# Two chained sequence-mixing layers on one core: another order inside the delta heads and the HGRN heads

## The chip, the cores and the metric

The kernel is one program on 1 core of a Trainium2 chip. The metric is the device time of one execution in microseconds. Three runs of the kernel before gave 3632.32, 3632.64 and 3636.35 us, a median of 3632.64 us.

## The reference, cut to what matters

Two blocks run one after the other on x of 512 tokens by 2048 channels, in float32.

The first block normalizes x and projects it to 12 groups of a gated delta rule (one query and key head each, two value heads each), a small cross attention over 256 memory rows (4 heads of 256) and gates. A short causal convolution and SiLU make q, k and v:

```python
qkv = jax.nn.silu(causal_depthwise_conv(p[..., :c_qkv], conv_w))
m = jnp.where(strict, beta[..., :, None] * kk * decay, 0.0) + jnp.eye(C)
sol = lax.linalg.triangular_solve(m, rhs, ...)        # u0, w
# over the chunks: u = u0 - w S;  o = q_dec S + (qk * decay) u;  S = cd * S + k_dec^T u
o = rms_norm(o, out_g); y = concatenate([mix, xa]) * silu(z); x = x + y @ w_out
```

The second block projects the normalized x to 4 mLSTM heads and 8 HGRN heads. An HGRN head is

```python
f_b = lb + (1 - lb) * sigmoid(hg_f);  logf = log(f_b);  k_b = (1 - lb) * sigmoid(-hg_f)
b = cumsum(logf);  A[t, j] = sum_e q[t, e] k[j, e] exp(b[t, e] - b[j, e])   for j <= t
o = A v + (q * exp(b)) S;   S = exp(g) * S + (k * exp(g - b))^T v
y_b = rmsnorm(o, hg_norm_w) * silu(hg_g)
```

An output projection, a gated embedding of p and a last norm end the block.

## The kernel before, in words

Activations lie transposed, channels on the 128 partitions and the 512 tokens on the free axis. Each weight tile is 2048 x 128. A projection of one tile is 16 parts (`gemm`, lines 379 to 395); a part is three 128x512 products, since weights and activations are cut into a high and a low half (lines 390, 391, 392). GpSimd cuts the weights of the next tiles (lines 358, 366), SyncE loads them. Tiles alternate between two PSUM banks, `gemm_ps`; a bank is free again when VectorE or ScalarE has moved the result out ("evict").

The work of a head ("mix") is woven into the projection of the next head's tiles. The function `interleave` makes one list of steps: each step has a weight, and it comes before the part at which the sum of the weights ahead of it is due. TensorE, VectorE and ScalarE all walk the same list, each in its own order of queue, and meet over semaphores. A step that waits on one engine holds up all that is behind it on that engine.

A delta head has 6 tiles (q, k, v, v, z, z; 96 parts) and the steps of `DN_STEPS`. "natural" transposes k and makes the products k k and k q; "values" transposes v; "transposed" turns the first inverse block. Then a block inverse is built in levels 1 to 6. Each level has a "half" (TensorE writes bankA, line 523; ScalarE copies it to T1) and a "whole" (TensorE writes bankB and bankC, lines 533 and 535; VectorE merges them with predicated copies, line 798), for each of the two value heads a = 0, 1. Whole 0 of level 1 also waits for `kd` and `ke`, which VectorE makes in its step "transposed". "solved" (lines 542, 547), four pairs "rest" and "output" (the chunks) and "head_out" follow. In "head_out" ScalarE squares the output, TensorE sums the squares of o and of q with a matrix of ones (lines 580, 581), ScalarE takes the square root, and VectorE divides and gates. ScalarE evicts tile c of q, k, v with a scaled copy, VectorE adds the three other taps of the convolution, and ScalarE then applies SiLU (`dn_trip` of ScalarE, from line 1646). The loop runs 11 heads; the last head is woven into the first six tiles of the output projection.

An HGRN head has 4 tiles (f, q, i, g; 64 parts) and the steps of `HG_STEPS`: a diagonal (line 685), levels 0 to 6 (VectorE makes exponents, ScalarE exponentiates in place in bankB, VectorE multiplies by q and k, TensorE multiplies, line 692, VectorE merges, line 1287), "hg_state" (transposes of kdt, line 703), "hg_mix" (line 709), "hg_next" (gates of the next head) and "hg_out" (lines 716, 718, 722). The loop runs 7 heads; the last is woven into two tiles of the second output projection.

The helper `op` of each engine is one line, so VectorE's operations are at line 792 and ScalarE's at line 1454. Table loads that the program asks for are at lines 1588, 1635 and 1829; others, at 1454, are put in by the compiler.

## Time and profile before

| | |
|---|---|
| median of the timed runs | 3632.64 us |
| the profiled execution, its own time | 3633.32 us |
| its span | 3631.5 us |
| TensorE busy | 3369.6 us, 93% |
| VectorE busy | 1534.2 us, 42% |
| ScalarE busy | 846.3 us, 23% |
| GpSimd busy | 1686.3 us, 46% |
| mean granted clock | 0.975 |

Engines in the rows: PE is TensorE's products, PEld its weight loads, DVE is VectorE, ACT ScalarE, POOL GpSimd. A row of a timeline begins with its start and its length in microseconds from the span's start; "x8" means eight instructions put together, and the square bracket gives how long the engine was idle before and what ended that. The ends of matmuls are modelled, so rows of PE overlap. A granted clock of 1.00 is 2.4 GHz, 0.50 is 1.2 GHz.

### The profile page before, as it was taken

Reading aid. Unit: us, or ns where it says so; the run is one execution under the profiler, and the core shown is the slowest. Engines: PE = TensorE matmul, PEld = TensorE weight load, DVE = VectorE, ACT = ScalarE, POOL = GpSimd, SP = SyncE. Lnnn points to the kernel's source line nnn. Section 1 sums busy time; section 2 is a strip of 40 time slices with the busy share of each in tenths; the row PEclk is TensorE's granted clock in tenths of the full one; section 3 lists DMA queues with packets and bytes.
Section 4 is the critical chain, followed back from the end, with each engine's and each line's share of the span. In section 5 each row is a group of like instructions: output and inputs, shape, how many; then the busy total and the mean of one; then the engine's idle time right before and its main releaser. Section 6 shows DMA issues by size and latency. Waiting matters only on the chain.

```text
span 3631.5 us, 47399 instructions
## 1 busy us (share of the span) xinstructions
PE 3369.6 (93%) x17232; PEld 2785.8 (77%) x17232; DVE 1534.2 (42%) x2049; ACT 846.3 (23%) x1269; POOL 1686.3 (46%) x1748
## 2 busy tenths in 40 slices
PE   8999989999999999999899998999988888879896
PEld 7777778788878877887688787777867777658685
DVE  7622244444543444444431214243355555531423
ACT  5412223322332233223310102111122322310111
POOL 0255623443343334334326666666644545437574
PEclk9999999999999999999899999999999999989998
DMA  6322211211111112112214223222222121232222
GB/s 235 117 82 87 93 53 52 69 60 50 64 69 58 52 64 69 41 63 69 93 64 174 81 97 134 87 104 92 92 76 73 64 72 61 98 115 100 73 100 81
DMA packets 53523, 306.68 MB, mean 84 GB/s; under 512 B 5044, under 2 KB 7220, under 8 KB 21844
## 3 DMA queue, kind: packets, MB, share of 16 engines
q1 hardware_dynamic: 33984, 247.48, 19.4%
q10 hardware_dynamic: 19476, 58.32, 4.3%
q8 instruction: 45, 0.74, 0.1%
q14 instruction: 18, 0.15, 0.0%
HBM read 284.74 MB, written 21.04 MB: 84 GB/s over the span
## 4 chain that ended last, share of the span: by engine, by line
PE 76%; DVE 12%; ACT 6%; issue 4%; DMA 1%; ACTq 0%; DVEq 0%; POOL 0%; POOLq 0%
PE gemm_ps L390 19%; PE gemm_ps L392 19%; PE gemm_ps L391 19%; DVE arena L792 8%; DVE arena L798 3%; ACT arena L1454 3%; PE bankC L535 3%; PE bankA L523 3%; PE bankB L533 2%; PE bankA L692 1%; ACT L1454 1%; PE bankB L580 1%; PE bankB L581 1%; DVE a_lo L792 1%; ACT a_hi L1454 1%
## 5 line engine op out<-in xcount | busy, mean ns | idle before, releaser
L390 PE MATMUL gemm_ps<-a_hi,w_hi 128*128 128x512 f32 (+1 forms) x3744 | 1512.2, 404 | 59.4 <-DVE a_lo L792 48.3
L392 PE MATMUL gemm_ps<-a_hi,w_lo 128*128 128x512 f32 (+1 forms) x3744 | 1446.7, 386 | 0.0
L391 PE MATMUL gemm_ps<-a_lo,w_hi 128*128 128x512 f32 (+1 forms) x3744 | 1444.3, 386 | 0.0
L366 POOL CAST w_hi<-w_raw 128x512 fp32r<-128x512 f32 x872 | 536.8, 658 | 1898.4 <-issue 1754.4
L358 POOL TENSOR_TENSOR w_lo<-w_raw,w_hi 128x512 fp32r<-128x512 f32 x872 | 1153.3, 1353 | 4.3
L390 PEld LDWEIGHTS gemm_ps<-a_hi,w_hi 128*128 128x128 f32 x3744 | 713.6, 191 | 216.2 <-issue 47.5
L392 PEld LDWEIGHTS gemm_ps<-a_hi,w_lo 128*128 128x128 f32 x3744 | 711.5, 190 | 143.5
L391 PEld LDWEIGHTS gemm_ps<-a_lo,w_hi 128*128 128x128 f32 x3744 | 714.3, 191 | 129.9 <-issue 10.1
L792 DVE TENSOR_TENSOR arena<-gemm_ps,arena 128x512 f32<-128x512 f32 (+3 forms) x145 | 96.0, 662 | 705.5 <-PE gemm_ps L392 699.4
L792 DVE RECIPROCAL arena<-arena 128x512 f32<-128x512 f32 (+2 forms) x70 | 172.8, 2468 | 352.2 <-ACT arena L1454 350.1
L1454 ACT ACTIVATE arena<-arena 128x512 f32<-128x512 f32 (+5 forms) x334 | 204.4, 612 | 404.3 <-DVE arena L792 390.9
L792 DVE TENSOR_TENSOR arena<-arena 128x512 f32<-128x512 f32 (+4 forms) x219 | 214.4, 979 | 66.5 <-ACT arena L1729 43.9
L535 PE MATMUL bankC<-arena 128*128 128x128 f32 x1152 | 210.9, 275 | 0.0
L523 PE MATMUL bankA<-arena 128*128 128x128 f32 x1152 | 161.5, 283 | 38.5 <-DVE arena L798 19.4
L523 PEld LDWEIGHTS bankA<-arena 128*128 128x128 f32 x1152 | 141.8, 192 | 71.6 <-DVE arena L798 46.5
L1454 ACT ACT_TABLE_LOAD x105 | 134.7, 1283 | 235.8 <-DVE arena L792 200.2
L533 PE MATMUL bankB<-arena 128*128 128x128 f32 x960 | 185.1, 274 | 0.0
L798 DVE COPY_PREDICATED arena<-con,bankB 128x512 f32<-128x512 uint32 x120 | 88.1, 734 | 225.9 <-PE bankC L535 222.9
L1454 ACT ACTIVATE arena<-bankA 128x512 f32<-128x512 f32 x144 | 86.2, 599 | 400.6 <-PE bankA L523 400.6
L535 PEld LDWEIGHTS bankC<-arena 128*128 128x128 f32 x1152 | 170.9, 192 | 2.1
L792 DVE SCALAR_TENSOR_TENSOR arena<-gemm_ps,arena 128x511 f32<-128x511 f32 x144 | 107.8, 748 | 142.6 <-ACT arena L1454 139.2
L533 PEld LDWEIGHTS bankB<-arena 128*128 128x128 f32 x960 | 154.5, 191 | 10.5
(155 smaller groups left out, 2238.2 us busy)
## 6 DMA issues: line engine op xcount, KB each, us to landing
w_raw<-w_stream SPq DMA_DIRECT2D x236, 1024.0 KB, 4.8
y_scratch<-arena ACTq DMA_DIRECT2D x20, 512.0 KB, 3.2
arena<-y_scratch ACTq DMA_DIRECT2D x15, 512.0 KB, 3.7
arena<-gc_scratch ACTq DMA_DIRECT2D x12, 512.0 KB, 3.5
arena<-x_t ACTq DMA_DIRECT2D x2, 2048.0 KB, 10.5
arena<-y_scratch ACTq DMA_DIRECT2D x1, 4096.0 KB, 25.5
x_scratch<-arena ACTq DMA_DIRECT2D x1, 4096.0 KB, 12.1
y_out<-arena ACTq DMA_DIRECT2D x4, 1024.0 KB, 3.9
```

Source lines behind the costliest of these rows:

```text
L358: return pool.tensor_tensor(part(w_lo, w, q), part(w_raw, w, q), part(w_hi, w, q).bitcast(F32), ALU.subtract)
L366: pool.tensor_copy(part(w_hi, w, q), part(w_raw, w, q)).then_inc(pool_step, 1)
L390: pe.matmul(o, hi, a_hi[:, k, 0:width], start=(k == 0), stop=False)
L391: pe.matmul(o, hi, a_lo[:, k, 0:width], start=False, stop=False)
L392: last = pe.matmul(o, lo, a_hi[:, k, 0:width], start=False, stop=(k == KT - 1))
L523: last = pe.matmul(quad(bankA)[:, a, n, :], NmT[:, a, n, :], X[:, a, n, :], start=True, stop=True)
L533: pe.matmul(quad(bankB)[:, a, n, :], XT[:, a, n, :], T1[:, a, n, :], start=True, stop=True)
L535: last = pe.matmul(quad(bankC)[:, a, n, :], T1[:, a, n, :], XT[:, a, n, :], start=True, stop=True)
L580: pe.matmul(bankB[:, a, :], ones, sqr[:, a, :], start=True, stop=False)
L792: d.did(make(*args), sem, value)
L798: d.did(make(*args), sem, value)
L1454: d.did(act.activation(dst, src, func, **kw), sem, value)
```

## The change

In the delta heads the weights of a level's four steps change, and with them their place: the second half comes one part later, directly ahead of whole 0. In "head_out" TensorE first adds the sums of q's squares for both a, without a wait, and then those of o. ScalarE holds the SiLU of an evicted tile back until the next step of the head is done (or, in "head_out", until the two squares are issued), and asks for the Sqrt table after the squares and no longer before them.

In the HGRN heads VectorE holds the eviction of a tile back until the next step is done, except that it comes first where the next step is "hg_next". The exponents of the state (h_b at a chunk's end minus h_b), their Exp on ScalarE and the product kdt move from inside "hg_state" to level 6 and to the start of "hg_state". The SiLU of the gate moves from the end of the head to the start of "hg_next", and ScalarE asks for the Exp table right after the square root of "hg_out".

```diff
-            + [(s, l, a, 0.75) for l in range(1, LEVELS) for s in ("half", "whole") for a in range(2)]
+            + [(s, l, a, w) for l in range(1, LEVELS)
+               for s, a, w in (("half", 0, 2), ("half", 1, 0), ("whole", 0, 1), ("whole", 1, 0))]
...
                 elif step[0] == "head_out":
                     for a in range(2):
+                        pe.matmul(bankB[:, a, :], ones, q_sq, start=True, stop=False)
+                    for a in range(2):
                         pe.wait_ge(s["o_sq"], 2 * j + a + 1)
-                        pe.matmul(bankB[:, a, :], ones, sqr[:, a, :], start=True, stop=False)
-                        pe.matmul(bankB[:, a, :], ones, q_sq, start=False, stop=True).then_inc(s["o_sum"], 1)
+                        pe.matmul(bankB[:, a, :], ones, sqr[:, a, :], start=False, stop=True).then_inc(s["o_sum"], 1)
...
+                    if l == LEVELS - 1:
+                        b3, p3 = h_bs.rearrange(blocks, n=NB), h_b.rearrange(blocks, n=NB)
+                        op(v.tensor_tensor, h_x[1].rearrange(blocks, n=NB), b3[:, :, P - 1:P].to_broadcast([P, NB, P]),
+                           p3, ALU.subtract, sem=s["h_kx"], value=j + 1)
                     v.wait_ge(s["h_ex"], LEVELS * j + l + 1)
...
                 elif step[0] == "hg_state":
+                    v.wait_ge(s["h_kxe"], j + 1)
+                    op(v.tensor_tensor, h_kdt, h_k, h_x[1], ALU.mult, sem=s["h_kdr"], value=j + 1)
                     merge(LEVELS - 1, j)
...
+            def hg_trip(g, j):                       # VectorE
+                held = None
+                for step in interleave(4, HG_STEPS):
                     if step[0] == "evict":
-                        hg_evict(step[1], g)
+                        held = step[1]
                     elif step[0] != "gemm":
+                        if step[0] == "hg_next" and held is not None:
+                            hg_evict(held, g)
+                            held = None
                         hg_mix(step, j, g)
+                        if held is not None:
+                            hg_evict(held, g)
+                            held = None
+                if held is not None:
+                    hg_evict(held, g)
...
+            def conv_silu(c, g):                     # ScalarE
+                slot, n = tile_at(W_DN, c, g, 6)
+                act.wait_ge(evicted[slot], n + 1)
+                op(cv[:, c, :], cv[:, c, :], ACT.Silu, s["silu"], 4 * g + c + 1)
...
                 elif step[0] == "head_out":
-                    act.preload_act_table(ACT.Sqrt)
                     act.wait_ge(s["o"], j + 1)
                     for a in range(2):
                         op(sqr[:, a, :], bankC[:, a, :], ACT.Square, s["o_sq"], 2 * j + a + 1)
+                    if held is not None:
+                        conv_silu(held, g)
+                    act.preload_act_table(ACT.Sqrt)
...
-                        act.wait_ge(evicted[slot], n + 1)
-                        op(o, o, ACT.Silu, s["silu"], 4 * g + c + 1)
+                        held = c
                     elif step[0] not in ("gemm", "evict"):
-                        dn_mix(step, j, g)
+                        dn_mix(step, j, g, held)
+                        if held is not None and step[0] != "head_out":
+                            conv_silu(held, g)
+                        held = None
...
-                if step[0] == "hg_next" and g is not None:
+                if step[0] == "hg_next":             # ScalarE
+                    if j is not None:
+                        slot, n = tile_at(W_HG, 3, j, 4)
+                        act.wait_ge(evicted[slot], n + 1)
+                        op(h_gate, hg_in, ACT.Silu, s["h_gs"], j + 1)
+                    if g is None:
+                        return
...
+                    if step[1] == LEVELS - 1:
+                        act.wait_ge(s["h_kx"], j + 1)
+                        op(h_x[1], h_x[1], ACT.Exp, s["h_kxe"], j + 1)
                 elif step[0] == "hg_state":
-                    act.wait_ge(s["h_kx"], j + 1)
-                    op(h_x[1], h_x[1], ACT.Exp, s["h_kxe"], j + 1)
                     act.wait_ge(s["h_kT"], j + 1)
...
                     op(h_rt, bankA[:, 0, :], ACT.Sqrt, s["h_ort"], j + 1, bias=eps[:, :], scale=1.0 / P)
+                    if g is not None:
+                        act.preload_act_table(ACT.Exp)
...
-                if tiles:
-                    slot, n = tile_at(W_HG, 3, g, 4)
-                    act.wait_ge(evicted[slot], n + 1)
-                    op(h_gate, hg_in, ACT.Silu, s["h_gs"], g + 1)
```

## Rows read from the trace of the kernel before

**Rows 1.** The page, part 1: busy time and share of the span.

```profile
PE 3369.6 (93%) x17232; PEld 2785.8 (77%) x17232; DVE 1534.2 (42%) x2049; ACT 846.3 (23%) x1269; POOL 1686.3 (46%) x1748
```

**Rows 2.** Windows: delta, then HGRN; busy per engine, PE clock, DMA share, GB/s.

```profile
425.00:1790.00 1365.00, 1293.24 (x7583) 1097.00 (x7582) 616.57 (x857) 395.87 (x649) 502.48 (x528) 0.98 0.17 60
...
2702.00:3158.00 456.00, 405.69 (x1959) 331.64 (x1960) 253.14 (x415) 119.28 (x159) 206.65 (x216) 0.97 0.19 67
```

**Rows 3.** TensorE's waits: releaser, total us, times, longest.

```profile
PE bankA L692 <- DVE arena L792: 29.9, 18, 2.1
PE bankB L580 <- ACT arena L1454: 29.0, 11, 2.6
PE bankB L703 <- DVE arena L792: 22.1, 8, 2.8
PE bankA L523 <- DVE arena L798: 19.4, 60, 0.7
PE bankA L523 <- ACT arena L1454: 19.1, 11, 5.1
```

**Rows 4.** Timeline of TensorE at a delta head's end.

```profile
660.03 1.58 PE L580 MATMUL bankB<-arena,con 128*128 128x512 f32 x2 [2.64 <-ACT arena L1454]
661.41 1.91 PE L581 MATMUL bankB<-arena,con 128*128 128x512 f32 x2
...
664.87 0.79 PE L390 MATMUL gemm_ps<-a_hi,w_hi 128*128 128x512 f32 x1
```

**Rows 5.** Timeline of ScalarE at the same place.

```profile
657.44 0.63 ACT L1454 ACTIVATE arena<-arena 128x512 f32<-128x512 f32 x1 [2.55 <-DVE arena L792]
658.09 1.28 ACT L1635 ACT_TABLE_LOAD   x1
659.38 1.23 ACT L1454 ACTIVATE arena<-bankC 128x512 f32<-128x512 f32 x2
```

**Rows 6.** Windows, columns as in rows 2: behind two waits, and undisturbed.

```profile
660.60:664.00 3.40, 3.40 (x6) 1.34 (x5) 0.00 (x0) 0.65 (x2) 1.00 (x1) 0.50 0.38 82
664.00:684.00 20.00, 20.00 (x87) 16.07 (x86) 10.61 (x7) 9.25 (x15) 7.83 (x8) 1.00 0.16 52
...
2806.80:2811.90 5.10, 5.10 (x18) 4.07 (x17) 0.93 (x1) 0.60 (x1) 3.30 (x3) 0.67 0.12 16
```

**Rows 7.** Timeline of TensorE in levels 1 to 4 of a delta head.

```profile
586.74 0.38 PE L533 MATMUL bankB<-arena 128*128 128x128 f32 x2
...
591.00 1.06 PE L523 MATMUL bankA<-arena 128*128 128x128 f32 x8
...
593.00 1.16 PE L523 MATMUL bankA<-arena 128*128 128x128 f32 x8 [0.25 <-DVE arena L798]
...
598.96 0.28 PE L523 MATMUL bankA<-arena 128*128 128x128 f32 x1
...
607.73 0.49 PE L523 MATMUL bankA<-arena 128*128 128x128 f32 x2 [0.65 <-DVE arena L798]
```

**Rows 8.** Timeline of VectorE ahead of level 1; last, in the first head.

```profile
580.29 3.27 DVE L792 TENSOR_TENSOR arena<-arena 128x8 f32<-128x8 f32 x2
583.60 2.48 DVE L792 TENSOR_TENSOR arena<-bankB,arena 128x1024 f32<-128x1024 f32 x2
...
455.77 1.42 DVE L792 TENSOR_TENSOR arena<-arena 128x8 f32<-128x8 f32 x2
```

**Rows 9.** Timeline of TensorE in HGRN: level 0, level 3.

```profile
2838.95 0.49 PE L692 MATMUL bankA<-arena 128*128 128x128 f32 x2 [2.06 <-DVE arena L792]
...
2853.22 0.60 PE L692 MATMUL bankA<-arena 128*128 128x128 f32 x3 [1.94 <-DVE arena L792]
```

**Rows 10.** Timelines of VectorE and ScalarE in HGRN.

```profile
2832.08 0.69 DVE L792 TENSOR_TENSOR arena<-arena 128x512 f32<-128x512 f32 x1
...
2835.39 1.28 ACT L1454 ACT_TABLE_LOAD   x1
...
2849.23 0.58 ACT L1454 ACTIVATE bankB<-bankB 128x512 f32<-128x512 f32 x1
```

More of the change, by code:

```diff
@@ L1336, in hg_mix @@
                                         else h_par[:, bass.ds(j, 1), 2:3].rearrange("p h c -> p (h c)")))
-                    b3, p3 = h_bs.rearrange(blocks, n=NB), h_b.rearrange(blocks, n=NB)
-                    op(v.tensor_tensor, h_x[1].rearrange(blocks, n=NB), b3[:, :, P - 1:P].to_broadcast([P, NB, P]), p3,
-                       ALU.subtract, sem=s["h_kx"], value=j + 1)
-                    v.wait_ge(s["h_kxe"], j + 1)
-                    op(v.tensor_tensor, h_kdt, h_k, h_x[1], ALU.mult, sem=s["h_kdr"], value=j + 1)
                     v.wait_ge(s["h_ebx"], j + 1)
@@ L1357, in hg_mix @@
                     op(v.tensor_tensor, h_y, h_rt, h_gate, ALU.mult, sem=s["h_yr"], value=j + 1)
-            def hg_trip(g, j, tiles=True, mix=True):
-                for step in interleave(4 if tiles else 0, HG_STEPS if mix else []):
+            def hg_trip(g, j):
+                held = None
+                for step in interleave(4, HG_STEPS):
                     if step[0] == "evict":
-                        hg_evict(step[1], g)
+                        held = step[1]
                     elif step[0] != "gemm":
+                        if step[0] == "hg_next" and held is not None:
+                            hg_evict(held, g)
+                            held = None
                         hg_mix(step, j, g)
+                        if held is not None:
[3 more added lines that the diff above has]
+                    hg_evict(held, g)
             v.sem_inc(s["h_yst"], 16)
@@ L1603, in store_head, with dn_mix @@
                 act.dma_start(y_rows.rearrange("a p t -> p a t"), yo[:, :, :]).then_inc(s["dy_stored"], 16)
-            def dn_mix(step, j, g=None):
+            def conv_silu(c, g):
+                slot, n = tile_at(W_DN, c, g, 6)
+                act.wait_ge(evicted[slot], n + 1)
+                op(cv[:, c, :], cv[:, c, :], ACT.Silu, s["silu"], 4 * g + c + 1)
+            def dn_mix(step, j, g=None, held=None):
                 if step[0] == "natural":
@@ L1646, in dn_trip @@
             def dn_trip(g, j, mix=True):
+                held = None
                 for step in interleave(6, DN_STEPS if mix else []):
                     if step[0] == "evict":
+                        if held is not None:
+                            conv_silu(held, g)
+                            held = None
                         c = step[1]
@@ L1659, in dn_trip @@
                         op(o, gemm_ps[slot][:, :], ACT.Copy, s["tapped"], 4 * g + c + 1, scale=cw[:, 4 * c + 3:4 * c + 4])
-                        act.wait_ge(evicted[slot], n + 1)
-                        op(o, o, ACT.Silu, s["silu"], 4 * g + c + 1)
+                        held = c
                     elif step[0] not in ("gemm", "evict"):
-                        dn_mix(step, j, g)
+                        dn_mix(step, j, g, held)
+                        if held is not None and step[0] != "head_out":
+                            conv_silu(held, g)
+                        held = None
                 if not mix:
@@ L1856, in hg_mix, with hg_trip @@
                     act.dma_start(y_row.rearrange("a p t -> p (a t)"), h_y).then_inc(s["h_yst"], 16)
-            def hg_trip(g, j, tiles=True, mix=True):
-                for step in interleave(4 if tiles else 0, HG_STEPS if mix else []):
+            def hg_trip(g, j):
+                for step in interleave(4, HG_STEPS):
                     if step[0] not in ("gemm", "evict"):
                         hg_mix(step, j, g)
-                if tiles:
-                    slot, n = tile_at(W_HG, 3, g, 4)
-                    act.wait_ge(evicted[slot], n + 1)
-                    op(h_gate, hg_in, ACT.Silu, s["h_gs"], g + 1)
-            hg_trip(0, None, mix=False)
             hg_mix(("hg_next",), None, 0)
```

## The prediction

> **What bounds the kernel now.** I read the page first: TensorE is busy 93% of the span [rows 1], so a change helps only where it takes an idle stretch, or a slow-clock stretch, out of TensorE's line. The windows by stage come next: the 12 delta heads take 1365 us and the 8 HGRN heads 456 us, at a mean granted clock of 0.98 and 0.97 [rows 2]; these two stages are all that the diff touches. Then TensorE's waits [rows 3]. In delta it waits 11 times, 29.0 us, for ScalarE ahead of the head's square sums (L580), 60 times, 19.4 us, for VectorE's merges ahead of a half (L523), and 11 times, 19.1 us, for ScalarE's copy of X (also L523). In HGRN it waits 18 times, 29.9 us, ahead of a level (L692) and 8 times, 22.1 us, ahead of the state's transposes (L703). A printed wait counts from the modelled end of the last product, which lies 0.16 past the next possible start (a product lasts 0.39 and starts repeat every 0.23: 87 products in a 20.00 us window at clock 1.00 [rows 6]). So I add 0.16 to each such wait. Last, the clock: behind the wait at L580 the window 660.6 to 664.0 is granted 0.50, which is 1.2 in place of 2.4 GHz, and the next window 1.00 [rows 6].
>
> **Delta, the head's end (11 heads in the loop).** TensorE could start at 660.03 - 2.64 - 0.16 = 657.23, and its next projection product starts at 664.87 [rows 4]: 7.64 us. ScalarE's row tells why: SiLU of tile 3 from 657.44 for 0.63, then the table load of 1.28, and only then the squares [rows 5]. Now the sums of q (always ready) go first, and the table load follows the squares. The title says that the squares precede a tile's SiLU; by the order of the steps they do not here: tile 3 ends after part 63, the step "output 3" comes at part 65 and releases the held SiLU, and "head_out" comes at part 68 with nothing held. So the SiLU still ends at 658.07. The first square (0.61) ends at about 658.7, while TensorE is in its two q sums until 657.23 + 1.71 = 658.94. No stall is left. Four 128x512 sums cost 0.85 each at full clock (two of them ran for 1.91 to the modelled end [rows 4], mostly at half clock), together 3.41. Saved: 7.64 - 3.41 = 4.2 us, of which 2.8 is the wait and 1.4 the half clock behind it. The wait alone, with the clock drop staying, would be 2.8. I take 4.2: the stage's mean clock, 0.98 [rows 2], leaves room for little more than these drops (3.4 us at half clock in 123 is a mean of 0.986), so the shorter waits cause none. The square root and VectorE's reciprocals move some 3 us ahead and end well before the next head; the load itself is now beside TensorE's sums.
>
> Weighed against the skill: the row shows the load lasting 1.28 with the square following 0.01 later [rows 5]. The Trainium skill ("ScalarE: Activation LUTs", What ACT_TABLE_LOAD costs) has a drain of about 1.38 on top, 2.66 per switch. Here the trace disagrees, and the sum goes by the row.
>
> **Delta, the dense blocks.** Order per level before: half0, part, half1, part, whole0, part, whole1. After: half0, two parts, half1 and whole0 together, part, whole1. A half's second head waits for merges that end 2.0 us after the last whole (591.00 to 593.00 [rows 7]). Half0 and one part give 1.59 of cover, half0 and two parts 0.81 + 0.78 + 0.69 = 2.28. So the wait of 0.25 + 0.16 goes, and one change between product kinds (about 0.1) with it: a level takes 7.43 in place of 598.96 - 591.00 = 7.96 [rows 7]. Whole0 now follows half1 at once, but needs only half0's copy, which is 1.5 us old. Level 4 starts after 8.77 instead (598.96 to 607.73, [rows 7]), because tile 1's taps sit before the merges. With the later half1 the merges of whole0 end just as TensorE asks: 7.43 here too. Levels 2 to 6 save 0.53 + 1.34 + 0.30 + 0.53 + 0.53 = 3.23.
>
> The entry. X's copy stood behind tile 0's SiLU and its load; now it goes ahead of them, and the first half starts when TensorE is there: (19.1 - 5.1) / 10 = 1.4, and 0.16, earlier [rows 3]. But whole0 of level 1 also needs VectorE's kd and ke, whose pair starts at 583.60 and takes 2.48 [rows 8]: 586.08. Nothing moves VectorE's chain, which hangs on the head's start. TensorE would be at whole0 at 584.96 and waits until about 586.15, against 586.74 before [rows 7]. Saved 0.59, between 0 (VectorE later) and 1.57 (VectorE not binding). So a new wait of 1.2 us stands before whole0: what is late next.
>
> Per head 3.23 + 0.59 + 4.2 = 8.0; times 11 = 88.2. The first head waited 5.1 for X [rows 3] where the others waited 1.41; its VectorE chain ends earlier (1.42 in place of 3.27 for the same two operations [rows 8]), so 3.4 more (0 to 3.7). The last head has only the levels: 5 x 0.53 = 2.6. **Delta: 94.2.**
>
> **HGRN (7 heads in the loop).** Three stalls of TensorE go [rows 3, 9].
> Level 0: 2.06 + 0.16. ScalarE ended the head with the gate's SiLU and then loaded the Exp table (2835.39 [rows 10]) before level 0's exponentials. The SiLU goes to "hg_next", where ScalarE is idle before its sigmoids, and the Exp load behind the square root, beside VectorE's reciprocal. After h_y (2832.08 + 0.69 [rows 10]) and its store's issue ScalarE needs one copy and one Exp, some 0.6 each: done at about 2834.7. VectorE's diagonal ends at 2835.0, its weights (0.88) at 2835.9; TensorE comes at 2838.95 - 2.22 = 2836.73. Saved 2.2.
> Level 3: 1.94 + 0.16. VectorE evicted tile 0 and did the exponents of level 4 before level 3's weights; now the eviction follows. The weights need ScalarE's Exp of 2849.23 + 0.58 [rows 10] and 0.88 of their own: 2850.8. TensorE comes at 2853.22 - 2.10 = 2851.1. Saved 2.1, with 0.3 to spare.
> State: 2.8 + 0.16 [rows 3], and in most heads a clock drop behind it: the window behind the wait has 0.67 of the clock, so 1.7 of its 5.1 us are lost [rows 6]; the 15 products in it take 5.12 where 15 x 0.23 would be 3.5, so I take 1.6. The difference, its Exp and the product kdt now run in level 6 and at the start of the state step, neither behind the eviction of tile 1 nor behind merge 6: ready some 5 us early. Saved 4.55.
> Together 8.9; times 7 = 62.3. The price: tile 2's eviction, once free, now waits behind "hg_out": h_y starts at 2832.08 and takes 0.69 [rows 10], the eviction another 0.72, so the bank is free at 2833.5, and the next head's first product starts at 2833.58. I cost it at 0; the nearest rows bound it at 0 and 0.7 a head.
> If a table load still opens each head although Exp is there, the row's 1.28 [rows 10] puts level 0's weights at 2836.9: 0.2 late, 1 us in all. The Trainium skill ("ScalarE activation tables: per-element evaluation and per-set limits", Table sets in the compiler and the runtime) says that loads are placed per block, which speaks for that load. With the 2.66 of the Trainium skill ("ScalarE: Activation LUTs", What ACT_TABLE_LOAD costs) for it the level would be 1.5 late, 11 us in all, so 3480. No row decides whether it stays.
>
> **HGRN's entry and last head.** Before head 0 TensorE stands until VectorE's chain is through, and the gate's SiLU, its load and the next load (0.63 + 2 x 1.28) lie in that chain: 3.2 saved (1.9 if only SiLU and one load go). In the last head the state's wait goes (2.6 + 0.16) and the Exp load at its start: 4.2 (2.6 to 5). Both follow through to the end, since the chain to h_y decides the second output projection. **7.4.**
>
> Sum: 94.2 + 62.3 + 7.4 = 163.9. The profiled run took 3633.3 (span 3631.5), so 3469.4; the median of the timed runs is 0.7 lower: **3469**. In head periods: a delta head goes from 122.9 to 114.9, an HGRN head from 65.1 to 56.2.
>
> **The rivals.**
> 1. *The stalls move and the clock goes on dropping* (17%). For it: two waits of 2.6 and 2.8 are followed by half clock [rows 3, 6], and delta's new wait of 1.2 may add to another. Against: 1.41 at the head's start is not (the stage's mean of 0.98 [rows 2] is no more than the stretch at the head's end explains). Price: 1.4 in 11 delta heads and 1.6 in 6 HGRN heads, 25 us: 3494.
> 2. *VectorE's chain at a delta head's start is longer or shorter* (12%). The two small-and-large products before kd took 3.27 in one head and 1.42 in another [rows 8], the longer time beside GpSimd's subtractions. If GpSimd's work falls otherwise, whole0 comes up to 1.85 later or 1.2 earlier, in 11 heads: 3489 or 3456. The Trainium skill ("SBUF — State Buffer", Who interferes with whom) says that a VectorE operation with two SBUF inputs and a GpSimd one that reads SBUF block each other, and that the earlier issue wins; the two rows agree with it.
> 3. *Half of it only* (6%): the head's end keeps its wait, for instance because the squares still come behind the load. Then 46 us stay: 3515.
> 4. *Slower* (2%): the eviction of HGRN's tile 2 behind "hg_out" holds TensorE at each head's start, for 0.7 by the rows. It decides against the change only from 164/7 = 23 us a head, 30 times what the rows allow.
>
> **How the numbers follow.** Forecast (3455 to 3480): 62%. The range 3450 to 3500 takes in it, rivals 1 and 2. A difference of 0.2% (7 us) is what a measurement can tell. All cases but the last, and a hundredth for a change that nets out, lie far below 3625; the last is 0.02, and 0.01 is left for a change that nets out, taken from the forecast: faster 0.97, same 0.01, slower 0.02.
>
> **What would show it.** Right: no wait at L580; L523 waits for neither VectorE nor ScalarE; a new wait of about 1.2 at L533 on VectorE, once a head; L692 and L703 without waits inside the loop; head periods near 115 and 56; the granted clock of both stages at 0.99 or 1.00. Wrong: half clock that persists in most heads, a wait at the first product of an HGRN head, or a wait at L581 for the squares.

## The result, and the profile after

The changed kernel took 3477.53 us (median of 4 runs, 3475.19 to 3479.34), the kernel before on the same chip 3632.48 us (4 runs, 3632.29 to 3636.35): a ratio of 0.9571, 95% interval 0.9554 to 0.9587. The forecast was 3469 (3450 to 3500), faster. The profiled execution took 3479.34 us, its span is 3477.5.

New lines of kernel.py: a projection product stands in L391 to L393 (before L390 to L392), the halves in L524 (L523), the wholes in L534 and L536 (L533, L535), q's sums in L580, o's in L583, HGRN's diagonal in L687 (L685), its levels in L694 (L692), the state's transposes in L705 (L703); VectorE's operations have L794 (L792), ScalarE's L1467 (L1454), GpSimd's L359 and L367.

The page, part 1, answers to [rows 1]: TensorE is busy 95% of a shorter span, with as many products.

```profile
PE 3317.2 (95%) x17232; PEld 2780.8 (80%) x17232; DVE 1532.1 (44%) x2049; ACT 854.1 (25%) x1275; POOL 1692.5 (49%) x1748
```

The windows of the two stages, columns as in [rows 2]: delta heads, then the HGRN heads of the loop. Both now show a granted clock of 1.00, where 0.98 and 0.97 stood.

```profile
430.00:1700.00 1270.00, 1252.20 (x7577) 1094.08 (x7576) 619.78 (x857) 396.54 (x651) 508.25 (x530) 1.00 0.18 64
2609.00:3007.00 398.00, 390.40 (x1961) 323.90 (x1960) 242.97 (x413) 130.19 (x168) 207.54 (x216) 1.00 0.22 78
```

TensorE's waits, columns as in [rows 3]. Of the five rows there, the waits at the square sums, at the halves (ScalarE's but for one of 1.6 us in the first head) and at the state's transposes are gone; 5.7 of 29.9 us are left at the HGRN levels. The row of L534 is new: VectorE at a delta head's first whole. L687 is the entry to the HGRN heads (before 10.7, once).

```profile
PE bankB L534 <- DVE arena L794: 12.1, 11, 2.0
PE bankB L687 <- DVE arena L794: 9.6, 1, 9.6
PE bankA L694 <- DVE arena L794: 5.7, 10, 0.9
```

A delta head's end, answering to [rows 4, 5]. TensorE goes from its last part into the two q sums and the two o sums (each sum counts as two in these rows); no row has a bracket, so there is no wait, and the next projection product starts 3.03 us after the first sum, against 7.64 between the same points before. ScalarE squares first and loads the square root's table beside the sums; the SiLU still precedes the squares, as the prediction said.

```profile
644.86 1.88 PE L580 MATMUL bankB<-arena,con 128*128 128x512 f32 x4
646.58 1.88 PE L583 MATMUL bankB<-arena,con 128*128 128x512 f32 x4
647.89 0.80 PE L391 MATMUL gemm_ps<-a_hi,w_hi 128*128 128x512 f32 x1
```

```profile
645.08 0.63 ACT L1467 ACTIVATE arena<-arena 128x512 f32<-128x512 f32 x1 [2.55 <-DVE arena L794]
645.80 1.23 ACT L1467 ACTIVATE arena<-bankC 128x512 f32<-128x512 f32 x2
647.04 1.28 ACT L1658 ACT_TABLE_LOAD   x1
648.34 1.41 ACT L1467 ACTIVATE arena<-bankB,eps_q 128x512 f32<-128x512 f32 x2
```

A delta head's start, VectorE and then TensorE (answers to [rows 7, 8]). Tile 0's taps, the two small-and-large products and the pair kd, ke follow each other without idle time, and TensorE's first whole waits 1.01 us for the end of that chain.

```profile
569.24 2.32 DVE L794 SCALAR_TENSOR_TENSOR arena<-gemm_ps,arena 128x511 f32<-128x511 f32 x3 [0.84 <-ACT arena L1467]
571.59 3.28 DVE L794 TENSOR_TENSOR arena<-arena 128x8 f32<-128x8 f32 x2
574.90 2.48 DVE L794 TENSOR_TENSOR arena<-bankB,arena 128x1024 f32<-128x1024 f32 x2
```

```profile
577.53 0.46 PE L534 MATMUL bankB<-arena 128*128 128x128 f32 x2 [1.01 <-DVE arena L794]
```

An HGRN head's start, ScalarE and then TensorE (answers to [rows 9, 10]). The Exp table is loaded at 2718.18, ahead of need (L1889), and loaded again at 2724.09, when the loop's next head opens. Level 0 waits 0.47 for what stands behind it.

```profile
2718.18 1.28 ACT L1889 ACT_TABLE_LOAD   x1
...
2724.09 1.28 ACT L1467 ACT_TABLE_LOAD   x1 [4.62 <-DVE arena L794]
2725.38 0.60 ACT L1467 ACTIVATE bankC<-arena 128x512 f32<-128x512 f32 x1
```

```profile
2727.65 1.05 PE L694 MATMUL bankA<-arena 128*128 128x128 f32 x7 [0.47 <-DVE arena L794]
```

Where the 154 us of span came from, by the first starts of the same lines of TensorE in both traces:

| stretch | before | after | difference | forecast |
|---|---|---|---|---|
| start to the first delta mix | 428.13 | 429.82 | +1.7 | 0 |
| first delta head | 133.36 | 122.97 | -10.4 | -11.4 |
| 10 further heads of the loop | 122.87 each | 114.63 each | -82.4 | -80.2 |
| last delta head and what follows, to the norm (L617) | 435.08 | 431.92 | -3.2 | -2.6 |
| mLSTM heads and entry of HGRN, to L685 | 476.86 | 477.51 | +0.7 | -3.2 |
| 7 HGRN heads | 65.1 each (the first 65.9) | 56.7 each (the first 58.2) | -57.9 | -62.3 |
| last HGRN head, to the second norm | 259.71 | 257.29 | -2.4 | -4.2 |

### The profile page after: what moved, and what is told of

The parts are those of the page before. It is cut to its first block, busy times and chain, and to the rows that moved or that the text cites. A ratio compares the mean times of both kernels' runs of the same rounds, so it can differ in the third digit from the quotient of the medians.

```text
span 3477.5 us, 47405 instructions
## 1 busy us (share of the span) xinstructions
PE 3317.2 (95%) x17232; PEld 2780.8 (80%) x17232; DVE 1532.1 (44%) x2049; ACT 854.1 (25%) x1275; POOL 1692.5 (49%) x1748
## 4 chain that ended last, share of the span: by engine, by line
PE 82%; DVE 10%; issue 3%; ACT 3%; DMA 1%; ACTq 0%; POOL 0%; DVEq 0%; POOLq 0%
PE gemm_ps L391 21%; PE gemm_ps L393 21%; PE gemm_ps L392 21%; DVE arena L794 8%; PE bankC L536 4%; PE bankB L534 3%; PE bankA L524 3%; ACT arena L1467 2%; PE bankA L694 1%; DVE a_lo L794 1%; DVE arena L800 1%; PE bankB L548 1%; PE bankC L574 1%; ACT a_hi L1467 1%; PE bankB L583 1%
## 5 line engine op out<-in xcount | busy, mean ns | idle before, releaser
L391 PE MATMUL gemm_ps<-a_hi,w_hi 128*128 128x512 f32 (+1 forms) x3744 | 1501.6, 401 | 60.4 <-DVE a_lo L794 49.3
L393 PE MATMUL gemm_ps<-a_hi,w_lo 128*128 128x512 f32 (+1 forms) x3744 | 1442.9, 385 | 0.0
L392 PE MATMUL gemm_ps<-a_lo,w_hi 128*128 128x512 f32 (+1 forms) x3744 | 1441.1, 385 | 0.0
L367 POOL CAST w_hi<-w_raw 128x512 fp32r<-128x512 f32 x872 | 543.1, 665 | 1738.1 <-issue 1593.2
L359 POOL TENSOR_TENSOR w_lo<-w_raw,w_hi 128x512 fp32r<-128x512 f32 x872 | 1153.4, 1354 | 4.3
L391 PEld LDWEIGHTS gemm_ps<-a_hi,w_hi 128*128 128x128 f32 x3744 | 711.3, 190 | 218.7 <-issue 46.3
L393 PEld LDWEIGHTS gemm_ps<-a_hi,w_lo 128*128 128x128 f32 x3744 | 709.5, 189 | 143.1
L392 PEld LDWEIGHTS gemm_ps<-a_lo,w_hi 128*128 128x128 f32 x3744 | 712.0, 190 | 131.7 <-issue 9.0
L794 DVE TENSOR_TENSOR arena<-gemm_ps,arena 128x512 f32<-128x512 f32 (+3 forms) x145 | 96.0, 662 | 632.2 <-PE gemm_ps L393 623.3
L794 DVE RECIPROCAL arena<-arena 128x512 f32<-128x512 f32 (+2 forms) x70 | 172.8, 2468 | 317.8 <-ACT arena L1467 315.6
L1467 ACT ACTIVATE arena<-arena 128x512 f32<-128x512 f32 (+5 forms) x334 | 204.5, 612 | 401.5 <-DVE arena L794 387.3
L794 DVE TENSOR_TENSOR arena<-arena 128x512 f32<-128x512 f32 (+4 forms) x219 | 212.6, 971 | 66.0 <-ACT arena L1756 43.9
L536 PE MATMUL bankC<-arena 128*128 128x128 f32 x1152 | 210.9, 275 | 0.0
L534 PE MATMUL bankB<-arena 128*128 128x128 f32 x960 | 186.1, 275 | 12.1 <-DVE arena L794 12.1
L1467 ACT ACTIVATE arena<-bankA 128x512 f32<-128x512 f32 x144 | 86.1, 598 | 391.4 <-PE bankA L524 391.3
L536 PEld LDWEIGHTS bankC<-arena 128*128 128x128 f32 x1152 | 169.9, 192 | 1.0
L534 PEld LDWEIGHTS bankB<-arena 128*128 128x128 f32 x960 | 150.0, 191 | 19.1 <-ACT arena L1467 11.7
L794 DVE SCALAR_TENSOR_TENSOR arena<-gemm_ps,arena 128x511 f32<-128x511 f32 x144 | 107.8, 749 | 126.5 <-ACT arena L1467 123.1
L524 PE MATMUL bankA<-arena 128*128 128x128 f32 x1152 | 152.1, 275 | 1.6 <-ACT arena L1467 1.6
L524 PEld LDWEIGHTS bankA<-arena 128*128 128x128 f32 x1152 | 146.2, 191 | 8.5 <-ACT arena L1467 2.0
```

The source lines that it names most:

```text
L359: return pool.tensor_tensor(part(w_lo, w, q), part(w_raw, w, q), part(w_hi, w, q).bitcast(F32), ALU.subtract)
L367: pool.tensor_copy(part(w_hi, w, q), part(w_raw, w, q)).then_inc(pool_step, 1)
L391: pe.matmul(o, hi, a_hi[:, k, 0:width], start=(k == 0), stop=False)
L392: pe.matmul(o, hi, a_lo[:, k, 0:width], start=False, stop=False)
L393: last = pe.matmul(o, lo, a_hi[:, k, 0:width], start=False, stop=(k == KT - 1))
L524: last = pe.matmul(quad(bankA)[:, a, n, :], NmT[:, a, n, :], X[:, a, n, :], start=True, stop=True)
```

## The experiments

Each is the changed kernel with one edit, timed beside the kernel before, which took 3633.8 to 3636.0 us (medians) on the chips of these runs. The line numbers of a run can be one or two off those of the change. The ratios to it have intervals of 0.0016 to 0.0018 on either side, about 6 us, so the times (medians of 4 runs) are read together with the spacing of the heads in the traces, which repeats to 0.05 us within a run.

| edit | us | ratio | delta head | HGRN head |
|---|---|---|---|---|
| the change | 3477.5 | 0.9571 | 114.63 | 56.70 |
| HGRN edits alone (e2) | 3574.2 | 0.9828 | 122.87 | 56.70 |
| no blocks (e3) | 3516.3 | 0.9665 | 117.87 | 56.70 |
| no held SiLU (e4) | 3501.9 | 0.9626 | 116.49 | 56.70 |
| old order of sums (e5) | 3495.7 | 0.9613 | 116.31 | 56.70 |
| old place of the load (e6) | 3488.4 | 0.9592 | 115.79 | 56.70 |
| both (e7) | 3526.1 | 0.9696 | 119.21, twice 117.49 | 56.70 |
| old gate (e10) | 3492.9 | 0.9606 | 114.64 | 58.38, twice 59.99 |
| Exp loaded at the entry (e11) | 3472.8 | 0.9549 | 114.63 | 55.95 |
| free evictions (e8) | 3502.8 | 0.9638 | 114.62 | 60.85, once 59.26 |
| old state (e9) | 3485.2 | 0.9585 | 114.63 | 57.61 |
| scans after GpSimd (e13) | 3477.6 | 0.9566 | 114.63 | 56.70 |
| e11 and late taps (e12) | 3458.1 | 0.9514 | 113.39 | 55.95 |

### Do the two stages add up? (e2)

```
-            + [(s, l, a, w) for l in range(1, LEVELS)
-               for s, a, w in (("half", 0, 2), ("half", 1, 0), ("whole", 0, 1), ("whole", 1, 0))]
+            + [(s, l, a, 0.75) for l in range(1, LEVELS) for s in ("half", "whole") for a in range(2)]
...
-                        held = c
+                        conv_silu(c, g)
```

and the edits of e7 besides.

> The change with every edit to the delta heads undone: new are only the edits to the HGRN heads and their table loads. Theory (the gains of the two stages add): the marks of the two traces give the delta heads 10.4 (first) + 82.4 (ten of the loop) + 3.2 (last) = 96.0 us of the 154, and HGRN 57.9 + 2.4 of it, so this kernel should be near 3632.5 - 60 = 3572 us, its delta heads 122.9 us apart as before and its HGRN heads 56.7. Rival (part of HGRN's gain hangs on what the delta stage left behind, its queues or the clock): the HGRN heads come out more than 1 us from 56.7, and the time is below 3560 or above 3584.

Measured 3574.2 us, delta heads as before to 0.01 us, HGRN heads as in the change. HGRN's gain does not hang on the delta edits. The delta edits alone were not run; but no edit to HGRN below (e8 to e11, e13) moves the delta heads by more than 0.01 us from 114.63, so the two stages are taken to add up.

### The dense blocks (e3)

Only the first hunk of e2.

> The change, but the dense tiles of a delta head are spread over its solve as before (weights 0.75 everywhere), so that halves and wholes each have fewer between them. Theory (the blocks cover VectorE's copies): TensorE's waits on the copies of levels 2 to 6 return, 3.23 us a head by the prediction's sum and 2.6 in the last head: 3477.5 + 11 x 3.23 + 0.6 = 3514 us, a head 118 us long. Rival (the chain at a head's start, not the order of tiles, is what gave the gain: VectorE now starts its levels earlier): waits of under 0.1 us at the levels and 3477 to 3490 us.

Measured 3516.3 us, heads 117.87 apart: 3.24 us a head. Four waits of 0.25 and one of 0.65, each with its 0.16, are 2.45 of it; the rest the sum put down to how the products follow each other, and no run takes it apart. The waits on the merges are back, in number and length those of [rows 3]:

```profile
PE bankA L523 <- DVE arena L799: 19.4, 60, 0.7
```

VectorE's earlier start does nothing for them: in e3 as before a level with 0.25 waits once, for a merge that ends a fixed time after the last whole.

### ScalarE's held SiLU (e4)

Only the second hunk of e2.

> The change, but ScalarE does a tile's SiLU right after its taps again instead of a step later. Theory (ScalarE's place in line matters): SiLUs of 0.63 us stand ahead of the copies that TensorE waits for; at level 0 0.5 us more a head and at level 3 up to 1.4 us, and the first head loses up to 4: about 3477.5 + 11 x 1.9 + 4 = 3502 us. Rival (every such SiLU lies beside dense tiles long enough to hide it): no TensorE wait grows, 3475 to 3481 us.

Measured 3501.9 us, 1.85 us a head and 5.4 more in the first. Two waits of TensorE on ScalarE take the place of the one on VectorE. The first half waits for the copy of X, at 579.55 behind tile 0's SiLU and its load. The second is at level 3, whose second whole needs the copy of its second half: at 601.93, behind tile 1's SiLU. TensorE, then ScalarE:

```profile
580.63 1.05 PE L524 MATMUL bankA<-arena 128*128 128x128 f32 x7 [1.40 <-ACT arena L1467]
...
602.58 0.49 PE L534 MATMUL bankB<-arena 128*128 128x128 f32 x2 [1.18 <-ACT arena L1467]
```

```profile
577.53 1.28 ACT L1467 ACT_TABLE_LOAD   x1 [2.54 <-DVE arena L794]
578.83 0.63 ACT L1467 ACTIVATE arena<-arena 128x512 f32<-128x512 f32 x1
579.55 1.02 ACT L1467 ACTIVATE arena<-bankC 128x1024 f32<-128x1024 f32 x1
...
601.21 0.63 ACT L1467 ACTIVATE arena<-arena 128x512 f32<-128x512 f32 x1 [2.46 <-DVE arena L794]
601.93 0.60 ACT L1467 ACTIVATE arena<-bankA 128x512 f32<-128x512 f32 x1
```

(1.40 + 0.16 + 1.18 + 0.16) - (1.01 + 0.16) is 1.73 of the 1.85. So the hold is what lets the blocks pay: with halves and wholes packed, a SiLU of 0.63 in the wrong place is a wait.

### The head's end: two edits and the clock (e5, e6, e7)

e5:

```
-                        pe.matmul(bankB[:, a, :], ones, q_sq, start=True, stop=False)
-                    for a in range(2):
                         pe.wait_ge(s["o_sq"], 2 * j + a + 1)
-                        pe.matmul(bankB[:, a, :], ones, sqr[:, a, :], start=False, stop=True).then_inc(s["o_sum"], 1)
+                        pe.matmul(bankB[:, a, :], ones, sqr[:, a, :], start=True, stop=False)
+                        pe.matmul(bankB[:, a, :], ones, q_sq, start=False, stop=True).then_inc(s["o_sum"], 1)
```

> The change, but TensorE sums a delta head's squares of o before those of q again; ScalarE loads its table behind the squares as in the change. Theory (the sums of q fill part of the wait for the squares, and what is left alone is too short to halve the clock): a wait of about 1.5 us returns in each head, 3477.5 + 11 x 1.5 = 3494 us. Rival (the clock drops behind that wait too): 1.5 + 1.6 us a head, 3511 us, with a half-clock stretch in each head.

e6:

```
                 elif step[0] == "head_out":
+                    act.preload_act_table(ACT.Sqrt)
                     act.wait_ge(s["o"], j + 1)
...
-                    act.preload_act_table(ACT.Sqrt)
```

> The change, but ScalarE loads the square root's table (1.28 us) ahead of a delta head's squares again; TensorE keeps the new order. Theory: the squares come 1.3 us later, of which the q sums and what slack there is hide a part: about 1.1 us a head, 3477.5 + 11 x 1.1 = 3490 us. Rival (that wait halves the clock again): 1.1 + 1.6 us a head, 3507 us.

e7 has both.

> The change, but a delta head's end is as before in both places: ScalarE loads the square root's table before its squares, and TensorE sums the squares of o before those of q. Theory (the head's end cost two waits and a stretch at half clock): 2.6 + 1.6 us each head return, with a half-clock stretch of 3.4 us behind them: 3477.5 + 11 x 4.2 = 3524 us. Rival (the clock's drop came from elsewhere, so only the waits return): 2.6 to 2.8 us a head, 3507 us, and no half-clock stretch in a head.

Measured: e5 1.68 us a head, with a wait of 1.42 in all 11 heads; e6 1.16, with a wait of 0.93; e7 4.58 in most heads, but 2.86 in two. 1.68 + 1.16 = 2.84 is e7 without the clock. The two kinds of heads of e7 stand side by side in its trace (windows from the end of one wait to the end of the next, columns as in [rows 2]):

```profile
650.24:769.47 119.23, 115.52 (x689) 99.88 (x689) 56.02 (x78) 35.42 (x59) 45.25 (x49) 0.99 0.18 62
769.47:886.95 117.48, 113.78 (x689) 99.29 (x689) 56.42 (x78) 35.41 (x59) 46.18 (x49) 1.00 0.17 62
```

Both windows start behind the same wait of 2.64 us and hold the same 689 products; in the second the clock is not halved and the head is 1.75 us shorter. That is the price of a drop, taken within one run. Behind e5's wait of 1.42 and e6's of 0.93 no head shows half clock. So each edit alone removes the drop as well: the first of them is worth its wait and 1.7, the second only its wait. The times agree: 3495.7, 3488.4 and 3526.1 against 3494, 3490 and 3524 expected.

### HGRN, the gate and the table load (e10, e11)

e10:

```
-                if step[0] == "hg_next":
-                    if j is not None:
...
-                        op(h_gate, hg_in, ACT.Silu, s["h_gs"], j + 1)
+                if step[0] == "hg_next" and g is not None:
...
-                        act.preload_act_table(ACT.Exp)
...
+                gate_silu(g)
```

> The change, but HGRN's gate goes through its SiLU at the end of the head before, as before the change, and the exponential's table is not loaded ahead. Theory (level 0 waits for ScalarE's first exponential, which stands behind the gate's SiLU and the table loads): 1.6 us a head more, 3477.5 + 7 x 1.6 + 1 = 3490 us, with TensorE's wait at level 0 back at 2.1 us. Rival (VectorE's chain of scans, not ScalarE, ends level 0's wait, as a table load still opens each head): 3476 to 3480 us.

Measured 3492.9 us. The wait at level 0 is 2.15 us, 1.68 a head; behind it the clock halves in two of the heads, which adds 1.6 each, and the entry's wait is 10.7 again. This run undoes two edits, the gate's place and the early load of the Exp table. As a load still opens each head of the change (2724.09), the 1.68 is put down to the gate's SiLU and the load that it needs; no run has one of the two edits without the other.

```profile
PE bankA L694 <- DVE arena L794: 18.6, 13, 2.2
PE bankB L687 <- DVE arena L794: 10.7, 1, 10.7
```

e11:

```
             hg_mix(("hg_next",), None, 0)
+            act.preload_act_table(ACT.Exp)
```

> The change, and one more load of the exponential's table ahead of the HGRN loop, so that the loop is entered from both sides with the same table. Theory (the load of 1.28 us that still opens each head is placed because the loop's entry has another table than its end): the load at the head's start goes, the wait of 0.48 + 0.16 us at level 0 with it: 3477.5 - 7 x 0.6 = 3473 us. Rival (a loop's body loads its table whatever it is entered with): the load of 1.28 us still stands at each head's start, 3476 to 3479 us.

Measured 3472.8 us: heads 55.95 apart, 0.75 less. The second load is gone: L1889 is followed by the store's issue and at once by the copy, and level 0 no longer waits.

```profile
2714.28 1.28 ACT L1889 ACT_TABLE_LOAD   x1
2719.43 0.34 ACTq L1892 DMA_DIRECT2D y_scratch<-arena  x1
2720.19 0.60 ACT L1467 ACTIVATE bankC<-arena 128x512 f32<-128x512 f32 x1 [4.63 <-DVE arena L794]
```

So in this loop the preload at the end counts only if the loop is entered with the same table. The Trainium skill ("ScalarE activation tables: per-element evaluation and per-set limits", Table sets in the compiler and the runtime) says that loads are placed per block; the trace agrees for the change, and e11 adds that a block whose entries agree gets none.

### HGRN, evictions and state: the wrong split (e8, e9)

e8:

```
-                        held = step[1]
+                        hg_evict(step[1], g)
```

> The change, but VectorE takes an HGRN tile out of its bank as soon as its turn comes again instead of after the next mask copy. Theory (at level 3 the copy that TensorE waits for stood behind a tile's eviction): the wait of 1.94 + 0.16 us at level 3 returns in each head, 3477.5 + 7 x 2.1 = 3492 us, HGRN heads 58.8 us apart. Rival (it was the freed table load and the moved state work that shortened the levels): heads 56.7 us apart and 3476 to 3480 us.

Measured 3502.8 us: 25 more, not 14.7. The wait at level 3 came back at its old size, once a head, but two things came with it: 0.22 us at the state, and half clock in five of the seven heads. Windows from one level-3 wait to the next:

```profile
2807.65:2868.51 60.86, 57.66 (x281) 47.11 (x281) 36.32 (x59) 18.60 (x24) 30.66 (x33) 0.97 0.21 73
2868.51:2927.75 59.24, 56.04 (x280) 45.96 (x281) 36.32 (x59) 18.60 (x24) 30.66 (x33) 1.00 0.21 75
```

Without a drop the hold is worth 59.26 - 56.70 = 2.56 us a head (2.48 of it are 1.94 + 0.16 at level 3 and 0.22 + 0.16 at the state), a drop another 1.6: 7 x 2.56 + 5 x 1.6 = 25.9. I had left the clock out of this expectation.

e9:

```
-                    v.wait_ge(s["h_kxe"], j + 1)
-                    op(v.tensor_tensor, h_kdt, h_k, h_x[1], ALU.mult, sem=s["h_kdr"], value=j + 1)
...
+                    op(v.tensor_tensor, h_x[1].rearrange(blocks, n=NB), b3[:, :, P - 1:P].to_broadcast([P, NB, P]), p3,
+                       ALU.subtract, sem=s["h_kx"], value=j + 1)
+                    v.wait_ge(s["h_kxe"], j + 1)
+                    op(v.tensor_tensor, h_kdt, h_k, h_x[1], ALU.mult, sem=s["h_kdr"], value=j + 1)
```

> The change, but HGRN's state factors (VectorE's subtraction, ScalarE's exponential, VectorE's product) are made after the last level again. Theory: TensorE's wait for them (2.79 + 0.16 us) returns in eight heads, and behind it the clock falls to half for 3.4 us in each head of the loop: 3477.5 + 8 x 3.0 + 7 x 1.7 = 3513 us, heads 61.4 us apart. Rival (the clock's drop hung on several waits of a head together, and the others are gone): no half-clock stretch in a head, 59.7 us apart, 3501 us.

Measured 3485.2 us: 7.6 more where the theory said 36 and the rival 24; heads 57.61 apart, no half clock. Both fell. The wait at L705 came back in eight heads, but at 0.7 us in the loop:

```profile
PE bankB L705 <- DVE arena L794: 7.7, 8, 2.6
```

VectorE's rows say why. Before the change, at the end of level 6:

```profile
2867.40 0.69 DVE L792 TENSOR_TENSOR arena<-gemm_ps,arena 128x512 f32<-128x512 f32 x1 [4.80 <-PE gemm_ps L392]
2868.23 0.73 DVE L1287 COPY_PREDICATED arena<-con,bankA 128x512 f32<-128x512 uint32 x1
2869.22 0.15 DVE L1335 COPY arena<-arena 128x1 f32 x1 [0.26 <-DVE arena L1287]
```

and in e9:

```profile
2751.48 0.74 DVE L1289 COPY_PREDICATED arena<-con,bankA 128x512 f32<-128x512 uint32 x1 [3.58 <-PE bankA L694]
2752.47 0.15 DVE L1337 COPY arena<-arena 128x1 f32 x1 [0.25 <-DVE arena L1289]
```

Before, VectorE stood 4.80 us for tile 1's last product and only then merged level 6 and went on to the state. In e9 it merges as soon as level 6's products are out, and the held eviction follows the state. So the wait of 2.77 + 0.16 falls by 2.0 through the hold alone and by 2.55 (to 0.22 + 0.16, e8) through the earlier state alone; the two edits cover each other, and only both bring it to nothing.

### The entry of HGRN (e13)

```
                     v.wait_ge(s["h_ln"], g + 1)
+                    if j is None:
+                        slot, n = tile_at(W_HG, 5)
+                        v.wait_ge(cut[slot], n + 1)
```

> The change, but before the first HGRN head VectorE starts its four scans only once GpSimd has made the low part of the sixth HGRN weight tile (its four subtractions end at 2606.98 in the trace after the change, the scans begin at 2603.30 and take 4.42 us; before the change they took 1.80). Theory (GpSimd's subtractions slow VectorE's scans when they overlap, which took most of the 3.2 us that the prediction gave the stage's entry): the scans start 3.8 us later and take 1.8 us, TensorE's wait there goes from 9.6 to about 10.8 us, and the time rises by only 1 us, to 3478.5. Rival (the scans are slower for another reason, their own operands or their place in line): they take 4.4 us again and the wait is 13.4 us.

Measured 3477.6 us, TensorE's wait 10.55. VectorE's last eviction and its scans in the change with the GpSimd row beside them, then VectorE's rows in e13:

```profile
2598.91 0.69 DVE L794 TENSOR_TENSOR arena<-gemm_ps,arena 128x512 f32<-128x512 f32 x1 [8.75 <-PE gemm_ps L393]
...
2603.30 4.42 DVE L794 TENSOR_TENSOR_SCAN arena<-con,arena 128x128 f32<-128x128 f32 x4
...
2601.47 5.51 POOL L359 TENSOR_TENSOR w_lo<-w_raw,w_hi 128x512 fp32r<-128x512 f32 x4
```

```profile
2597.63 0.69 DVE L794 TENSOR_TENSOR arena<-gemm_ps,arena 128x512 f32<-128x512 f32 x1 [8.75 <-PE gemm_ps L393]
...
2605.56 1.80 DVE L794 TENSOR_TENSOR_SCAN arena<-con,arena 128x128 f32<-128x128 f32 x4 [3.65 <-POOL w_lo L359]
```

The same four scans take 1.80 alone and 4.42 beside the subtractions. Counted from the eviction, e13 starts them at 7.93 in place of 4.39 and ends them at 9.73 in place of 8.81: 3.5 later at the start, 0.9 at the end, which is what TensorE's wait grew by. The Trainium skill ("SBUF — State Buffer", Who interferes with whom) says that a VectorE operation with two SBUF inputs and a GpSimd operation that reads SBUF hold each other up; these rows agree, 0.65 us for each scan.

### A version that beats both (e12)

```
-            def dn_evict(c, g):
-                if c == 0:
+            def dn_evict(c, g, part=None):
+                if c == 0 and part != "taps":
...
-                if c >= 4:
+                if c >= 4 or part == "copy":
...
+                        held = mix and step[1] == 0
+                        dn_evict(step[1], g, "copy" if held else None)
...
                         dn_mix(step, j, g)
+                        if held:
+                            dn_evict(0, g, "taps")
+                            held = False
...
                         dn_mix(step, j, g, held)
+                        if held == 0 and step[:3] != ("half", 1, 1):
+                            continue
...
+            act.preload_act_table(ACT.Exp)
```

> The change, with the exponential's table loaded once more ahead of the HGRN loop (3472.8 us in an earlier run, this edit alone), and a new one: at a delta head's start VectorE and ScalarE only free tile 0's bank, and do its taps and its SiLU later, behind the step of the transposed tile and behind level 1's second half. Theory (the new wait of 1.01 + 0.16 us at the first whole comes from tile 0's taps standing ahead of the chain of a head's start): the wait goes, 3472.8 - 11 x 1.17 - 1 = 3459 us, delta heads 113.5 us apart. Rival (the taps come into the way of a copy of levels 1 or 2 instead, or the chain is bound by its own products): heads 114.6 us apart or more, 3471 to 3480 us.

Measured 3458.1 us (3457.22 to 3459.84), 19.5 below the change and 176 below the kernel before on the same chip (3633.83); heads 113.39 apart. VectorE's pair kd, ke ends at 567.44, and TensorE's wholes of level 1 follow its halves at 570.74 without a wait (one of 0.9 is left in the first head). VectorE, then TensorE:

```profile
562.79 2.13 DVE L794 TENSOR_TENSOR arena<-arena 128x8 f32<-128x8 f32 x2
564.96 2.48 DVE L794 TENSOR_TENSOR arena<-bankB,arena 128x1024 f32<-128x1024 f32 x2
...
567.97 2.32 DVE L794 SCALAR_TENSOR_TENSOR arena<-gemm_ps,arena 128x511 f32<-128x511 f32 x3
```

```profile
569.85 1.05 PE L524 MATMUL bankA<-arena 128*128 128x128 f32 x8
570.74 0.39 PE L534 MATMUL bankB<-arena 128*128 128x128 f32 x2
```

## Why the prediction was right, point by point

- **What bounds the kernel.** Right. The gain is TensorE's waits and its half-clock stretches in two stages, and outside them the marks moved by 1.7 us at most.
- **The head's end, 4.2 us.** By e7 4.58: waits 2.86 (2.8 forecast), the clock 1.7 (1.4). That the clock's drop hung on this wait alone, read from the stage's mean of 0.98, held: no delta head of the change shows half clock. Which edit did it: either, by e5 and e6.
- **The dense blocks, 3.23.** By e3 3.24, from the same waits. What the prediction did not price is that they need ScalarE's hold: without it 1.85 a head come back (e4).
- **The entry of a head, 0.59.** The head gained 8.24 in all, so 8.24 - 4.58 - 3.24 = 0.42 is left. The new wait at the first whole was forecast at about 1.2 from VectorE's two rows and is 1.01 + 0.16. e12 shows its cause: tile 0's taps ahead of the chain.
- **First head.** 10.4 in place of 11.4. The chain waits 2.0 there, not 1.2, X's copy still holds TensorE for 1.6, and a half-clock stretch stands at 442.09 in this run; the runs of e9 and e11, without one there, have 11.8 and 11.9. The kernel before had a half-clock stretch of its own in this head, at 459.2 behind the wait of 5.1, which the forecast did not count; so its 11.4 is close partly by luck.
- **HGRN, 8.9 a head; measured 8.3.** Level 0: 1.59 of the 2.22, since the load stays, the case that the prediction named and could not decide. It put level 0 at 0.2 late for it (1 us in all); it is 0.47 + 0.16 late, and e11 without the load gains 0.75 a head. That is the mis-sized term. Level 3: its wait is gone, and e8 brings it back at 1.94 + 0.16. State: the wait of 2.95 is gone, but it was credited to the moved state work; the hold of the eviction accounts for 2.0 of it by itself (e9). The sum was right and the split wrong. The clock's 1.6 came, 1.6 by e8 and e10. But the drops did not all hang on the state's wait, as the prediction had it: of the eight in the seven heads of the kernel before, five follow it and three follow the 1.94 at level 3. With the wait of level 3 or of level 0 back alone (e8, e10), drops come back in part of the heads.
- **Tile 2's eviction, 0.** Right; no wait stands at a head's first product.
- **Entry and last head, 7.4; measured 1.8.** This step failed. At the entry (3.2 forecast) ScalarE's work did go out of VectorE's way, and the scans start 3.7 earlier against TensorE, but they then ran beside GpSimd and took 2.6 longer (e13), which the prediction had put at nothing. TensorE's wait fell by 1.05. The rest of this stretch lost 1.7: TensorE waits 3.32 us for VectorE at the first mLSTM tile in both kernels, and in the change the clock is halved for 3.41 us behind that wait, while before it is not. Twelve microseconds from there, before and after, columns as in [rows 2]:

```profile
2269.68:2281.68 12.00, 12.00 (x53) 9.96 (x54) 1.34 (x2) 0.00 (x0) 5.58 (x6) 1.00 0.25 88
```

```profile
2175.44:2187.44 12.00, 12.00 (x46) 9.76 (x47) 0.65 (x1) 0.00 (x0) 4.86 (x4) 0.86 0.24 88
```

In the last head the waits did fall, as forecast, by 4.4 us: TensorE is idle for 33.1 in place of 37.5 (window less busy time, below). But it runs or waits at half clock for 41.0 us there in place of 34.1, and of the 4.4 only 2.4 are left. The prediction counted no clock at either place. The windows of that stretch, before and after:

```profile
3158.45:3418.16 259.71, 222.23 (x953) 178.21 (x952) 80.08 (x110) 34.31 (x52) 138.21 (x144) 0.93 0.31 106
```

```profile
3006.88:3264.17 257.29, 224.21 (x954) 180.28 (x952) 82.57 (x111) 33.03 (x51) 138.01 (x144) 0.92 0.31 108
```

- **The rivals.** The clock going on dropping (17%) did not come about in the heads. It was a near thing, by e8 and e10: with one wait of 1.94 or 2.15 left per head it came about in five heads of seven and in two of six. VectorE's chain at the head's start did come out as forecast, at 3.28 and 2.48. Half only and slower did not occur.

The profiled execution came 9.9 us above the sum's 3469.4. By the table, 4.4 are HGRN's heads, 5.6 its entry and last head, 1.7 a half-clock stretch in the cross attention at 332.87, ahead of all that was changed; the delta heads gave 1.8 more than forecast.

## What to carry to other kernels

When a wait goes because two edits both move it, undo each alone before crediting one: here one alone took 2.0 and the other alone 2.6 of 2.9 us. An engine whose work fills gaps between another's steps (taps, SiLUs, evictions) should do it behind the step that the bound engine waits for, and the gain of packing that engine's work depends on it. A wait may cost more than its length through the clock: at a delta head's end the first of two edits took 1.7 us of half clock away besides its share of the wait, the second only its share.

## What the runs showed of the hardware

- **The clock behind short waits.** TensorE's clock halved for 3.41 us behind waits of 2.64 us in 11 of 11 heads (before) and 9 of 11 (e7), behind 2.15 in 2 of 6 (e10), behind 1.94 in 5 of 7 (e8), and in no delta head whose longest wait was 1.42 (e5), 1.40 (e4) or 1.01 (e6), 10 heads each, the first left out. A drop cost 1.6 to 1.75 us. In the kernel before, each HGRN head waits 1.94 at level 3 and 2.77 to 2.79 some 18 to 20 us later at the state: the clock fell behind the first in three of the seven heads, behind the second in five, and behind both only in the first head. The sixth head, where it fell behind the shorter wait (3048.40) and not behind the longer (3068.3), columns as in [rows 2]:

```profile
3049.90:3053.30 3.40, 3.40 (x10) 2.66 (x9) 3.09 (x7) 0.98 (x2) 3.33 (x3) 0.50 0.00 0
3068.30:3071.70 3.40, 3.40 (x17) 2.91 (x18) 1.25 (x1) 0.60 (x1) 3.40 (x3) 1.00 0.00 0
```

What decides between places with the same wait these runs do not settle.
- **A table load** takes 1.28 us in all 143 places of the change's trace, and an activation that waits for nothing else follows 0.01 to 0.02 later. Loading the Exp table ahead of need at the HGRN loop's end did not spare the load at its start until the loop was also entered with it (e11).
- **VectorE's scans** (128x128) take 0.45 us each alone and 1.10 beside GpSimd's subtractions (e13).
